# Hybrid encoder layer: filter spectra made inside the chunk loop, low parts written over the weight slabs, wide merge, folded Fourier branch

## The reference, cut to what matters

```
xn = rmsnorm(h);  z = xn @ w_in                                # 2048 x 16384
y_a = x2 * fftconv(x1 * fftconv(u, k0), k1)  * silu(gate_a)    # u, x1, x2: width-3 convolution of z's columns
y_b = real(fft2(fin over 272 positions and 256 channels))      * silu(gate_b)
y_c = neighbourhood_attention(q, k, v, bias)                   * silu(gate_c)
m   = sum over branches of sigmoid(merge_b) * (y_b @ w_b)      # three 1024 x 2048, gates from z
out = rmsnorm(h + m @ w_out), meta tokens dropped
```

## Time and profile before

| | us |
|---|---|
| median of 3 runs | 1236.78 (1232.86 to 1237.75) |
| the profiled execution | 1234.91 |
| its span, first to last instruction | 1233.1 |
| PE busy | 1185.0 (96%), 9310 matmuls |
| DVE busy | 724.6 (59%) |
| ACT busy | 525.6 (43%) |
| POOL busy | 83.9 (7%) |
| mean granted PE clock | 0.991 |

### The profile page before, as it was taken

The page is one execution under the profiler, slowest core; times in us unless marked ns, Lnnn a source line. Parts: engine busy times, 40 slices in busy tenths (PEclk is TensorE's granted clock), DMA queues, the critical chain, the costliest instruction groups (busy, mean ns, idle before and its releaser), DMA issues.

```text
span 1233.1 us, 20883 instructions
## 1 busy us (share of the span) xinstructions
PE 1185.0 (96%) x9310; PEld 1128.2 (91%) x9310; DVE 724.6 (59%) x882; ACT 525.6 (43%) x589; POOL 83.9 (7%) x110
## 2 busy tenths in 40 slices
PE   3898999999999999999999999999999999999996
PEld 1344999999999999999999999999999999999996
DVE  5667567755777566765677646454444544444554
ACT  5566335433444335343344444433334333343342
POOL 3221500030000300002000000000000000000000
PEclk9988999999999999999999999999999999999998
DMA  9043744355434544334453465545555455556551
GB/s 299 5 170 101 247 154 147 128 186 181 161 132 145 189 171 155 137 136 183 147 180 105 152 248 175 197 175 187 189 175 199 174 185 191 176 198 244 208 196 74
DMA packets 32369, 209.69 MB, mean 170 GB/s; under 512 B 4119, under 2 KB 4472, under 8 KB 9224
## 3 DMA queue, kind: packets, MB, share of 16 engines
q1 hardware_dynamic: 25976, 184.80, 41.9%
q0 software_dynamic: 6304, 23.56, 5.7%
HBM read 198.65 MB, written 9.70 MB: 169 GB/s over the span
## 4 chain that ended last, share of the span: by engine, by line
PE 83%; DVE 9%; ACT 4%; issue 2%; DMA 1%; SPq 0%; ACTq 0%; DVEq 0%
PE ps L556 27%; PE ps L558 26%; PE ps L557 26%; ACT w_hi L862 2%; DVE w_lo L1128 2%; PE ps L596 1%; PE ps L561 1%; PE ps L582 1%; DVE hm L1200 1%; DMA xin<-x 1%; PE ps L654 1%; DVE sd L1204 1%; DVE sd L1203 1%; DVE prod L1270 1%; DVE prod L1271 1%
## 5 line engine op out<-in xcount | busy, mean ns | idle before, releaser
L1128 DVE TENSOR_TENSOR w_lo<-raw,w_hi 128x2048 fp32r<-128x2048 f32 x168 | 391.7, 2332 | 397.7 <-ACT w_hi L862 397.4
L556 PE MATMUL ps<-xn_hi,w_hi 128*128 128x256 f32 (+2 forms) x2048 | 582.9, 285 | 1.5 <-DVE w_lo L1128 1.5
L558 PE MATMUL ps<-xn_hi,w_lo 128*128 128x256 f32 (+2 forms) x2048 | 581.3, 284 | 0.0
L557 PE MATMUL ps<-xn_lo,w_hi 128*128 128x256 f32 (+2 forms) x2048 | 580.6, 284 | 0.0
L862 ACT ACTIVATE w_hi<-raw 128x2048 fp32r<-128x2048 f32 x166 | 317.7, 1914 | 492.5 <-PE ps L558 492.3
L556 PEld LDWEIGHTS ps<-xn_hi,w_hi 128*128 128x128 f32 x2048 | 386.9, 189 | 3.6 <-issue 2.4
L558 PEld LDWEIGHTS ps<-xn_hi,w_lo 128*128 128x128 f32 x2048 | 387.0, 189 | 0.0
L557 PEld LDWEIGHTS ps<-xn_lo,w_hi 128*128 128x128 f32 x2048 | 386.0, 188 | 0.0
L556 PE MATMUL ps<-yb_hi,w_hi 128*128 128x256 f32 x384 | 108.9, 284 | 1.1 <-DVE yb_lo L1128 1.1
L558 PE MATMUL ps<-yb_hi,w_lo 128*128 128x256 f32 x384 | 108.8, 283 | 0.0
L557 PE MATMUL ps<-yb_lo,w_hi 128*128 128x256 f32 x384 | 108.7, 283 | 0.0
(11 more groups left out here) (248 smaller groups left out, 1237.5 us busy)
## 6 DMA issues: line engine op xcount, KB each, us to landing
raw<-w_stream SPq DMA_DIRECT2D x168, 1024.0 KB, 4.8
raw<-tables SPq DMA_DIRECT2D x4, 1024.0 KB, 20.1
kspec_grid<-kstage POOLq DMA_DIRECT2D x4, 1024.0 KB, 4.6
kspec<-kspec_grid POOLq DMA_DIRECT2D x8, 512.0 KB, 4.7
branch_y<-ystage POOLq DMA_DIRECT2D x12, 256.0 KB, 3.9
y_raw<-branch_y POOLq DMA_DIRECT2D x3, 1024.0 KB, 5.1
xin<-x SPq DMA_DIRECT2D x2, 1024.0 KB, 7.4
absd<-decay POOLq DMA_DIRECT2D x4, 512.0 KB, 9.4
```

The source lines that it names most:

```text
L556: mm(out_ap, a_hi, b_hi, start=first, stop=False)
L557: mm(out_ap, a_hi, b_lo, start=False, stop=False)
L558: return mm(out_ap, a_lo, b_hi, start=False, stop=last)
L1128: return V.tensor_tensor(dst, src, hi.bitcast(F32), ALU.subtract)
```

## The change

Nothing of what is computed changes; where and in which form it is done does.

- Stage 2 is gone. The work for one filter order of one chunk is a group g (8 in all, 2c and 2c+1 for chunk c). Each engine has calls for it in the chunk loop, on ACT and DVE ahead of the split of that step. The product with w4 is made in fp32r with stacked high and low parts. Lags are ordered even first and odd behind; half the bins are computed from both halves (`filter_x`, `filter_y`, 256 columns each) and mirrored bins are their difference (`both_bins`). Spectra stay in SBUF.
- Tables come already split from the host, on POOL's queue.
- `w_lo` has four places and lies over `raw`: the low part is written where the slab was. A slab is loaded when PE has used the slab four before it.
- Merge: tokens stationary, 512 columns of weights moving, slabs of 512 rows x 512 columns; the sum is then transposed by PE (32 transposes in all, `turn_merged`). Output projection with 512 columns as well.
- Fourier branch: `fold_fin` on DVE makes sums and differences of mirrored positions, and 12 of 28 matmuls in `fnet_tokens` fall away; `fnet_channels` has 130 columns instead of 258 for two of three tiles.
- Smaller: the mean square of the meta rows on DVE, tanh written into `gate`, half of the final store on ACT's queue, `make_bias` ahead of the stores of a chunk on POOL.

The core of the diff:

```diff
+            for w in range(4):
+                sp.dma_start(raw[:, w, :], w_stream[w]).then_inc(w_landed[w], 16)
+            for w in range(4, NW):
+                sp.wait_ge(slab_used, w - 3)
+                sp.dma_start(raw[:, w % 4, :], w_stream[w]).then_inc(w_landed[w % 4], 16)
...
@@ POOL, for c in range(1, CH)
                 load_bias_rows(c)
-                second_order(c - 1)
+                load_filter(2 * c)
+                pool.wait_ge(smax_done, c * HC)
+                make_bias(c)
                 store_y(c - 1, 0, ya_done)
                 store_y(c - 1, 2, yc_done)
-                pool.wait_ge(smax_done, c * HC)
-                make_bias(c)
-                pool.wait_ge(y_full, c * 6)
-                load_spectrum(c, 0)
+                load_filter(2 * c + 1)
                 store_y(c - 1, 1, yb_done)
...
@@ PE
+            def make_h4(g, tt):
...
+                mm(out_ap, hid_s[:, p:p + n], w4_hi[:, :, :].rearrange("p d n -> p (d n)"), start=True, stop=False)
+                mm(out_ap, hid_s[0:HID, p:p + n], w4_lo[0:HID, :, :].rearrange("p d n -> p (d n)"), start=False,
+                   stop=True).then_inc(h4_mm, 1)
+            def even_or_odd(g, tt, done):
+                bank = (4 if g == 0 else 6) + (tt == 0)
+                if tt == 0:
+                    pe.wait_ge(sdlo_done, 3 * g + 3)
+                    pe.wait_ge(h4_read, 3 * g + 2)
+                else:
+                    pe.wait_ge(h4_read, 3 * g + 3)
+                for ri in range(2):
+                    out_ap = ps[:, bank, CC * ri:CC * ri + CC]
+                    col = 256 * tt + 128 * ri
+                    three(out_ap, filt_hi[:, col:col + 128], filt_lo[:, col:col + 128], sd_hi[:, tt, ri, :],
+                          sd_lo[:, tt, ri, :], True, False)
+                    col += FSTACK
+                    last = stacked(out_ap, filt_hi[0:STACK, col:col + 128], sd_rest[0:STACK, ri, :], False, True)
+                last.then_inc(done, 1)
...
@@ PE, behind slab t of chunk c
+                    if c == 0:
+                        if t == 0:
+                            pe.wait_ge(hid_done, 1)
+                            make_h4(0, 0)
+                            make_h4(0, 1)
+                        if t == 1:
+                            make_h4(0, 2)
+                        if t == 2:
...
+                            filter_x(0)
+                            filter_y(0)
+                            filter_f(0)
+                        if t == 3:
+                            make_h4(1, 0)
+                            make_h4(1, 1)
+                        if t == 4:
+                            make_h4(1, 2)
+                        if t == 5:
+                            filter_x(1)
+                            filter_y(1)
+                            filter_f(1)
+                    else:
+                        if t == 0:
+                            filter_f(2 * c)
+                        if t == 1:
+                            make_h4(2 * c + 1, 0)
+                            make_h4(2 * c + 1, 1)
+                        if t == 2:
+                            make_h4(2 * c + 1, 2)
+                        if t == 3:
+                            filter_x(2 * c + 1)
+                        if t == 4:
+                            filter_y(2 * c + 1)
+                        if t == 5:
+                            filter_f(2 * c + 1)
...
+                    if c + 1 < CH:
+                        if t == 16:
+                            make_h4(2 * c + 2, 0)
+                            make_h4(2 * c + 2, 1)
+                        if t == 17:
+                            make_h4(2 * c + 2, 2)
+                        if t == 18:
+                            filter_x(2 * c + 2)
+                        if t == 19:
+                            filter_y(2 * c + 2)
...
@@ ACT and DVE, in each step
                 for t in range(S1):
-                    split(slot_main(c, t + 2), t % 2, c * S1 + (t + 2))
+                    filter_step(c, t)
+                    split(c * S1 + t + 2)
...
@@ ACT, filter_step for c > 0
+                    if t == 2:
+                        sd_high(a, 0)
+                        envelope(a, 2)
+                        sd_high(a, 1)
+                    if t == 3:
+                        sd_high(a, 2)
+                    if t == 4:
+                        keep_x(a)
+                    if t == 6:
+                        keep_f(a)
...
@@ DVE
+            def sum_and_difference(g, tt):
...
+                V.tensor_tensor(hm[0:n, :, :].rearrange("p d n -> p (d n)"), ps[0:n, (4 if g == 0 else 6) + (tt == 1), :],
+                                env.rearrange("p d n -> p (d n)"), ALU.mult).then_inc(h4_read, 1)
+                dve.wait_ge(h4_read, m + 1)
+                if m:
+                    dve.wait_ge(sdlo_done, m)
+                V.tensor_tensor(sd[0:n, 0, :], hm[0:n, 0, :], hm[0:n, 1, :], ALU.add)
+                V.tensor_tensor(sd[0:n, 1, :], hm[0:n, 0, :], hm[0:n, 1, :], ALU.subtract).then_inc(sd_done, 1)
...
@@ DVE, filter_step for c > 0
+                    if t == 0:
+                        both_bins(2 * c)
+                        weights4_low(a)
+                    if t == 2:
+                        sum_and_difference(a, 0)
+                        sd_low(a, 0)
+                        sum_and_difference(a, 1)
+                        sd_low(a, 1)
+                    if t == 3:
+                        sum_and_difference(a, 2)
+                        sd_low(a, 2)
+                    if t == 5:
+                        both_bins(a)
+                if c + 1 < CH:
+                    if t == 15:
+                        weights4_low(b)
+                    if t == 17:
+                        sum_and_difference(b, 0)
+                        sd_low(b, 0)
+                        sum_and_difference(b, 1)
+                        sd_low(b, 1)
+                    if t == 18:
+                        sum_and_difference(b, 2)
+                        sd_low(b, 2)
+            def fold_fin(c, src, b):
...
+                V.tensor_copy(fi[:, :, NM + 128:L], mirror[:, :, 0:128])
+                link(V.tensor_copy(fi[:, :, 7:14], mirror[:, :, 128:135]))
+                V.tensor_copy(fi[:, :, 14:16], src[:, :, 0:137:136])
+                V.tensor_tensor(fi[:, :, NM:NM + 128], src[:, :, 1:129], fi[:, :, NM + 128:L], ALU.add)
...
@@ PE, merge and output
+            def wide_slab(w, pair, a_hi, a_lo, k0, count, p0):
...
+                for tt in range(2):
+                    toks = slice(p0 + 128 * tt, p0 + 128 * tt + 128)
+                    for k in range(4):
+                        cols = slice(WB * k, WB * k + WB)
+                        last = three(ps[:, pair + tt, :], a_hi[:, k0 + k, toks], a_lo[:, k0 + k, toks], hi[:, cols],
+                                     lo[:, cols], k0 + k == 0, k0 + k == count - 1)
```

More of the change, by code:

```diff
@@ L68 @@
 BRANCHES = (0, 2, 1)
[L69 removed]
+NG_F = 2 * CH
 TWO_PI = 2.0 * math.pi
@@ L74, with rounded, two_parts, both @@
 CLAMP = 3.1415925
+FPOS = np.concatenate([np.arange(256, L), np.arange(0, 256, 2), np.arange(1, 256, 2)])
+FSTACK = 4 * 128 + 4 * NM
+def rounded(x):
+    bits = np.ascontiguousarray(x, np.float32).view(np.uint32).astype(np.uint64)
+    return (((bits + 0x7FF + ((bits >> 12) & 1)) >> 12) << 12).astype(np.uint32).view(np.float32)
+def two_parts(main, rest):
+    def both(m):
+        x = m.astype(np.float32)
+        hi = rounded(x)
+        return hi, rounded(x - hi)
+    hi, lo = both(main)
+    if rest is None:
+        return hi, lo
+    rest_hi, rest_lo = both(rest)
+    under = np.zeros((128, rest.shape[1]), np.float32)
+    under[0:NM], under[32:32 + NM], under[64:64 + NM] = rest_hi, rest_lo, rest_hi
+    return np.concatenate([hi, under], axis=1), lo
 def constants():
     pos = np.arange(L, dtype=np.float64)
[L80 to L102, removed]
+    bins = np.concatenate([np.arange(128, 144), np.arange(128), np.arange(L - 1, 143, -1)]).astype(np.float64)
+    om = TWO_PI * (bins + 0.5) / FFT_N
+    sign = 1.0 - 2.0 * (bins % 2)
     half = (pos[:HL, None] + 0.5) * om[None, :]
@@ L853, in _ @@
+            for i in range(JW):
+                pair = pair_free(("out", i))
+                for q in range(4):
+                    pe.wait_ge(mlo_done, q + 1)
+                    wide_slab(w, pair, m_hi, m_lo, 4 * q, KT, 0)
+                    w += 1
+                    if i == 0 and q == 1:
+                        turn_merged(JW - 1)
         @block.scalar
@@ L1103, in _, with squares @@
+                    if j and t == 2:
+                        merged_high(j - 1)
+                    if t % 6 == 3:
+                        gated(j, t // 6)
+            def squares(i, tt):
+                act.wait_ge(h_sum, 2 * i + tt + 1)
+                A(fjunk[:, tt, WB * i:WB * i + WB], h[:, tt, WB * i:WB * i + WB], ACT.Square,
+                  accum_out=fsq[:, tt, i:i + 1]).then_inc(f_sq, 1)
```

(16 more changed lines are left out.)

1071 lines of the change are left out of this document (539 added, 532 removed).

## The result

The changed kernel takes **1255.58 us** (median of 4 runs, 1254.84 to 1256.54), the kernel before 1236.88 (median of 4, 1232.86 to 1237.75): ratio **1.0158**, 95% interval 1.0135 to 1.0181. It is slower by 1.6%; forecast were 1252 us, with a chance of 0.56 for slower. The profiled span is 1254.7 us, predicted 1248.5. Of all the runs of this document one, the second of e_best, took 1887.64 us at a mean granted clock of 0.563, and it is left out of that kernel's median.

What follows compares the result with a forecast made beforehand. PE was taken as the bound (83% of the chain). Terms -87.0 (loop start), +33.9 (PE filter work), +56.1 (waits), +20.7 (clock), -8.3 (merge and output) gave +15.4: median 1252 us, range 1190 to 1268.

Steps and rivals of the forecast that it cites:

- Loop start: Chunk loop begins when x is transposed, at 36.0 (between 34 and 40) instead of 123.0: -87.0 us.
- The waits: Chunk loop: PE waits 60.7 us for late ACT and DVE work, replacing 4.6 us of idle time: +56.1 us.
- step 3, chunks 1 to 3: PE waits before `filter_x` for the third lag tile, 7.0 us, three times: +21.0 us.
- bias beside softmax, chunks 0 to 2: `make_bias` starts beside the split of slab 15, with softmax behind it: 1.5 us each, +4.5 us (bounds 0 and 2.1 each).
- The prediction's signs: If right: PE gaps of 5 to 9 us behind slabs 3 and 18, chunk 0's 2 and 5; loop 36 to 742.
- The clock: Half clock behind each of nine long PE gaps in the loop, 2.3 us each: +20.7 us.
- PE work in the loop: Eight filter groups add 39.6 us of matmuls, the Fourier fold removes 1.4 us per chunk: +33.9 us.
- Merge and output: 512-column matmuls at 0.232 us plus 32 transposes, 495.4 against 505.0 us; taken as -8.3 us.
- Rival C: Wide matmuls in merge and output bring nothing or cost: 0.240 for 512 columns, +7.7 us, time 1268; chance 0.10.
- Rival A: Slack in DVE and ACT hides the loop's filter work, no waits: time 1173; chance 0.08.
- Rival B: Half the filter work hidden: waits 38 us, five cold gaps, loop start 34, time 1218; chance 0.25.
- Rival D: Slabs land late in the first 40 us, beside the tables: up to 10 us more, 1262; chance 0.10.

Runs made afterwards that it cites:

- e_best: Changed kernel with filter work laid out by when its parts are ready, plus three small reorderings (Fourier-bin copies, Fourier fold, bias): 1188.75 us, ratio 0.9614 to the kernel before.
- e_rows: Changed kernel with the second matmul of each filter-lag product on 128 rows instead of 64: 1242.75 us.
- e_warm: Changed kernel with throwaway PE matmuls in the gap ahead of each group's first filter transform: 1240.63 us, ratio 1.0033 to the kernel before.
- e_two: Changed kernel with ACT copying the odd group's folded Fourier bins and DVE folding the Fourier projection earlier, bias left in place: 1232.48 us.
- e_best2: e_best with 128 rows in the lag products, the bias moved, and chunk 0's folded bins transformed behind its last forward transform: 1172.57 us, ratio 0.9472 to the kernel before.
- e_narrow: Changed kernel with two matmuls of 256 columns for each of 512 in merge and output projection: 1269.76 us.
- e_three: Changed kernel with the two edits of e_two, and POOL making the bias behind the two stores of y: 1240.8 us.

## Why the prediction was right

Its time was 3.6 us off, and the mechanism is the one forecast: filter work in the loop that makes PE wait at the named steps, and a lowered clock behind the waits. The sizes of its terms were less good than the sum. Step by step:

- *Loop start*: 36.0 predicted, 38.15 measured (+2.1).
- *The waits*: 60.7 predicted, 54.8 measured (the four rows of the waits above), kind by kind:

| place | predicted | measured |
|---|---|---|
| chunk 0, steps 2 and 5 | 5.8, 9.4 | 4.97, 8.60 |
| step 3, chunks 1 to 3 | 7.0 | 6.02 |
| step 18, chunks 0 to 2 | 3.7 | 2.44 to 2.46 |
| step 6, chunks 1 to 3 | 1.6 | 1.83 to 1.85 |
| bias beside softmax, chunks 0 to 2 | 1.5 (steps 13, 14) | 1.62 (step 14) |
| step 16, all chunks | 0.9 | 1.21 to 1.43 |

  The count by hand of two engines' orders, one operation behind the other, came within 1.3 us at each place. Its part on ACT and DVE is nearly exact: at step 3 of chunk 1 the chain ends 19.85 us behind slab 1 (245.67 to 265.52), counted were 19.8. What differs is when PE gets there, after 13.9 us and not 12.8, because three products stand in between with 0.38 us of open weight loads each. In e_rows, without these, the gaps are 6.06, 9.65, 6.30, 2.7 to 3.0, 1.85, 1.62 and 1.2 to 1.4 us, and with three new ones of 0.54 they add up to 60.7 us. So the waits were too long in the count because the work of PE was too short in it: the two errors are for the most part one. The prediction's signs named gaps of 5 to 9 us at step 18 as well; its own count had 3.7, and 2.4 came.
- *The clock*: 20.7 for nine long gaps. For eight of them e_warm measured 15.4, 1.9 each instead of 2.3; behind the ninth, the 1.16 us ahead of the first slab, the granted clock stays at 1.00. What the sum had not: short gaps cost clock too, 13.6 us by the windows, and e_two got 15.0 back. Together some 30, 10 more than predicted.
- *PE work in the loop*: +33.9 predicted. Where nothing waits it is right (a chunk of e_best2 is 8.1 us longer than before; 9.9 - 1.4 = 8.5 predicted). In the changed kernel it was 9 us short: 24 products whose two weight loads lie open, 2 x 0.19 us each (in e_best2 these products have 128 rows). The price of the earlier trace rows was taken for matmuls of a form that no row showed and no bound was given for it.
- *Merge and output*: -8.3 predicted, -16 measured. 512 columns took 0.230 and 0.2275, not 0.232, over 2112 matmuls 5 us; PE idles 0.15 us there and not 2; and the sum had taken -8.3 where its own prices gave -9.6 (495.4 against 505.0). Rival C was wrong in both halves. What made it look likely, the 0.120 of the earlier trace rows, held for 256 columns and tokens stationary, and e_narrow has it again; 512 columns of that form are cheaper than 512 of the other.
- *Sum*: the errors are +2.1 at the start, -5.9 in the waits, +10 for the clock, +9 for the weight loads and -8 in the merge: +7, against 6.2 in the span. The loop ended at 756 and not at 742, and the shorter merge hid half of that. The errors nearly cancel, and that is luck: the time was met closer than the terms deserve.

Rival A (all hidden) was priced at 1173 us, and e_best2, in which the order is the only large difference beside the 9 us, takes 1172.6; this closeness too is in part luck, since 8.4 us of waiting that A did not have stand against 7.7 us that the merge gave beyond its price. The prediction's point against A, that the order is written out and not chosen by readiness, was the deciding one. Rival B fails on each of its parts: 55 us of waits and not 38, a loop from 38 and not 34, and a clock that did fall behind all three steps 18. Rival D is refuted by the waits: no slab came late.

## What to carry to other kernels

A stage with idle engines is worth folding into a dense loop only if its parts are placed where their inputs are ready: here the same work in the same loop gave +1.6% or, by order alone, -3.9% (e_best), and -5.3% with one operand's rows changed and the order mended once more (e_best2). Write down for each consumer when its three or four producers finish, engine by engine, before moving anything, and price a gap of TensorE, a short one too, at its length and up to some 2 us more; whether the 2 us come is read from the granted clock behind it, since not every gap brought them. Price a matmul by a row of its own form, rows included; columns below 256 and a mix of 64 and 128 rows don't follow the row of the neighbour.

## What the runs showed of the hardware that was not expected

- *Short gaps can lower the clock, and length alone does not decide.* Behind the gap of 1.42 us at 378.90 the rows of the changed kernel have a granted clock of 0.82 and then 0.50, the 1.2 GHz level (PE had been busy up to that gap, and the sparse stretch of open weight loads followed it):

```profile
380.00:381.00 1.00, 1.00 (x6) 0.58 (x5) 1.00 (x1) 0.35 (x2) 0.00 (x0) 1.00 1.09 426
381.00:382.00 1.00, 1.00 (x3) 0.37 (x2) 0.97 (x2) 0.00 (x0) 0.00 (x0) 0.82 0.87 315
382.00:384.00 2.00, 2.00 (x10) 1.89 (x10) 1.93 (x6) 0.00 (x0) 0.00 (x0) 0.50 0.27 109
```

  In e_rows, without the open loads, slab matmuls behind the same gap (1.43 us at 372.00) start 0.118 apart (374.36, 374.47, 374.59), at full clock. On the other side, e_best has the open loads behind a gap of only 0.53 us (349.09), and the clock falls (first row below), but e_two has the same, at 369.00 with 0.55 us, and it stays at 1.00. And behind the gap of 1.62 us at step 14 it stays in the changed kernel each of three times (second row, at 360.05), while behind the 1.83 to 1.85 us of step 6 it falls each time:

```profile
352.00:355.00 3.00, 3.00 (x14) 2.74 (x14) 2.90 (x7) 0.00 (x0) 0.00 (x0) 0.50 0.56 224
...
360.00:366.00 6.00, 5.95 (x48) 5.91 (x49) 3.37 (x7) 3.37 (x4) 1.17 (x3) 1.00 0.41 161
```

  In e_rows three gaps of 2.7 to 3.0 us at step 18 brought no lowered clock either; in the changed kernel three of 2.4 us did. What PE does around a gap may play a part, but the runs give no rule for it.
- *POOL's additions stop DVE's, they don't slow them*: 0.41 us became 4.10 beside 3.59 us of POOL (e_three), 0.42 became 4.41 beside 3.64 (e_best). The Trainium skill (SBUF — State Buffer, "Who interferes with whom") says that a DVE instruction with two inputs in SBUF contends with a GpSimd instruction that reads SBUF, and that the contention is an exclusive lock. The trace agrees, and shows more: DVE came free only when four of POOL's instructions in a row were over (214.70 against 214.42, and 56.45 against 56.16).
- *130 columns cost nearly as much as 256*: 0.112 and 0.118 us.
- *Left open*: what decides whether a short gap lowers the clock; and whether the earlier `keep_x(1)` frees the 3.42 us in chunk 0 of e_best2.
